# Six tiles of 344 tokens in two interleaved streams over one weight ring, for a hybrid decoder layer on eight cores

## The reference, cut to what matters

```python
D_MODEL = 1024; BATCH = 8; SEQ = 2048; DEC_BATCH = 128; PLE_DIM = 256
GLA_HEADS = 4; GLA_DV = 128; GLA_DK = 64; GLA_RANK = 16; CONV_WIDTH = 512; D_FF = 2816

def swiglu(x, w_gate, w_up, w_down):
    return (jax.nn.silu(x @ w_gate) * (x @ w_up)) @ w_down

def token_mixer(u, s0, conv0, w_in, w_gate_up, b_gate, gla_norm_g, conv_w, w_out):
    z = u @ w_in
    q, k, v, g, r, cb, cc, ch = jnp.split(z, points, axis=-1)
    gate_logit = (r @ w_gate_up + b_gate)
    log_a = jax.nn.log_sigmoid(gate_logit) / GLA_GATE_NORM
    o, s_new = gla_chunked(q, k, v, log_a, s0)   # S_t = diag(a_t) S_{t-1} + k_t^T v_t, o_t = q_t S_t
    o = rms_norm(o, gla_norm_g) * jax.nn.silu(g)
    full = jnp.concatenate([conv0, cc * ch], axis=1)
    y = sum(conv_w[j] * full[:, j:j + t_len] for j in range(CONV_K))
    out = jnp.concatenate([o, cb * y], axis=-1) @ w_out
    return out, s_new, full[:, -(CONV_K - 1):]

def decoder_layer(x, p, s0, conv0, ng, ...):
    h = x + 0.5 * rms_norm(swiglu(rms_norm(x, ng[0]), f1_gate, f1_up, f1_down), ng[1])
    mix, s_new, conv_new = token_mixer(rms_norm(h, ng[2]), s0, conv0, ...)
    h = h + rms_norm(mix, ng[3])
    h = h + 0.5 * rms_norm(swiglu(rms_norm(h, ng[4]), f2_gate, f2_up, f2_down), ng[5])
    gate = jax.nn.sigmoid(rms_norm(h, ng[6]) @ w_ple_gate)
    return h + rms_norm((p @ w_ple_proj) * gate, ng[7]), s_new, conv_new
```

## Time and profile before

| | |
|---|---|
| median of 3 runs | 2049.12 us (2028.93 to 2090.03) |
| span of the profiled execution, slowest core (core 5) | 2001.6 us |
| spans of the eight cores | 1986.7 to 2001.6 us |
| PE busy | 1718.5 us, 8,050 matmuls |
| DVE, ACT, POOL busy | 779.6, 657.8, 240.2 us |
| moved by DMA | 417.88 MB, mean 209 GB/s |

### The profile page before, as it was taken

How to read it: one execution, slowest core, us unless ns; L and a number is a source line. 1 busy time by engine, 2 the same in 40 slices (tenths; PEclk the granted TensorE clock), 3 DMA queues, 4 the chain that set the end, 5 groups by cost and what they waited for, 6 DMA issues and landing times.

```text
span 2001.6 us, 24196 instructions; the slowest of 8 cores (1986.7 to 2001.6 us)
## 1 busy us (share of the span) xinstructions
PE 1718.5 (86%) x8050; PEld 1375.0 (69%) x8050; DVE 779.6 (39%) x1338; ACT 657.8 (33%) x1274; POOL 240.2 (12%) x458
## 2 busy tenths in 40 slices
PE   5997879978988789979979789859997967799985
PEld 4885768856866668747858678647885757678865
DVE  2514526245513445045413355144513444234134
ACT  2124452253123441262233432352224341222243
POOL 1110101110110111101110111100110101001110
PEclk9997989989997899979988899979997985599986
DMA  9984759858893559849874558754663658346644
GB/s 257 312 254 122 201 155 297 253 173 253 285 279 106 168 185 296 256 162 289 261 222 158 189 203 255 225 179 169 219 195 114 206 198 273 138 148 224 189 140 143
DMA packets 77918, 417.88 MB, mean 209 GB/s; under 512 B 11203, under 2 KB 11860, under 8 KB 42726
## 3 DMA queue, kind: packets, MB, share of 16 engines
q0 software_dynamic: 65264, 396.88, 63.5%
q1 hardware_dynamic: 12534, 19.45, 3.5%
HBM read 405.55 MB, written 10.75 MB: 208 GB/s over the span
## 4 chain that ended last, share of the span: by engine, by line
PE 76%; ACT 8%; DVE 6%; issue 5%; DMA 3%; DVEq 0%; POOL 0%; ACTq 0%; POOLq 0%
PE ps_bank L287 66%; PE ps_bank L612 5%; PE ps_bank L300 3%; DMA sb_wslot<-f1a 3%; ACT sb_tmpa L318 2%; PE ps_bank L970 1%; ACT sb_sq L318 1%; DVE sb_big L321 1%; ACT sb_rs L318 1%; ACT sb_hgb L697 1%; DVE sb_xn L451 1%; ACT sb_xn L477 1%; DVE sb_Sst L326 1%; DVE sb_tmpb L326 1%; DVE sb_om L321 1%
## 5 line engine op out<-in xcount | busy, mean ns | idle before, releaser
L287 PE MATMUL ps_bank<-sb_xn,sb_wslot 128*128 128x512 f32 (+1 forms) x3456 | 829.1, 397 | 19.8 <-DVE sb_tmpa L321 10.4
L287 PEld LDWEIGHTS ps_bank<-sb_xn,sb_wslot 128*128 128x128 f32 x3456 | 653.2, 197 | 169.9 <-issue 27.0
L287 PE MATMUL ps_bank<-sb_big,sb_wslot 128*128 128x512 f32 x1408 | 336.4, 397 | 0.0
L287 PEld LDWEIGHTS ps_bank<-sb_big,sb_wslot 128*128 128x128 f32 x1408 | 262.0, 188 | 61.1
L318 ACT ACTIVATE sb_tmpa<-sb_tmpa 128x512 f32<-128x512 f32 (+1 forms) x216 | 133.4, 618 | 427.2 <-DVE sb_tmpa L321 427.0
L451 DVE TENSOR_TENSOR sb_xn<-sb_xn,sb_rs 128x512 fp32r<-128x512 f32 (+1 forms) x104 | 65.9, 644 | 489.4 <-ACT sb_rs L318 467.0
L321 DVE TENSOR_TENSOR sb_tmpa<-ps_bank,sb_rs 128x512 f32<-128x512 f32 (+1 forms) x216 | 144.6, 670 | 201.3 <-ACT sb_rs L318 126.2
L321 DVE TENSOR_TENSOR sb_tmpb<-ps_bank,sb_rs 128x512 f32<-128x512 f32 x176 | 121.2, 689 | 149.0 <-PE ps_bank L287 149.0
L612 PE MATMUL ps_bank<-sb_xn,sb_wslot 128*128 128x512 f32 x384 | 109.6, 453 | 45.1 <-DMA sb_wslot<-f1a 23.7
L321 DVE TENSOR_TENSOR sb_big<-sb_tmpb,sb_tmpa 128x512 fp32r<-128x512 f32 x176 | 121.9, 692 | 38.5 <-ACT sb_tmpa L318 24.4
L612 PEld LDWEIGHTS ps_bank<-sb_xn,sb_wslot 128*128 128x128 f32 x384 | 85.1, 224 | 69.0 <-issue 47.8
(11 more groups left out here) (130 smaller groups left out, 1483.6 us busy)
## 6 DMA issues: line engine op xcount, KB each, us to landing
sb_wslot<-f1a POOLq DMA_DIRECT2D x88, 1024.0 KB, 8.3
sb_wslot<-f2a POOLq DMA_DIRECT2D x88, 1024.0 KB, 6.9
sb_wslot<-f1b POOLq DMA_DIRECT2D x64, 704.0 KB, 5.6
sb_wslot<-f2b POOLq DMA_DIRECT2D x64, 704.0 KB, 5.5
sb_wslot<-wca POOLq DMA_DIRECT2D x20, 1024.0 KB, 6.5
sb_wslot<-wo POOLq DMA_DIRECT2D x20, 1024.0 KB, 6.8
sb_wslot<-wpg POOLq DMA_DIRECT2D x20, 1024.0 KB, 6.6
sb_wslot<-wv POOLq DMA_DIRECT2D x10, 1024.0 KB, 8.5
```

The source lines that it names most:

```text
L287: ins = e.matmul(out.ap, a.ap, b.ap, start=(first and i == 0), stop=(last and i == n_ - 1))
```

## The change

The 2,064 tokens of a core become six tiles of 344; the sample's 16 tokens are the last columns of the last tile, so they need no matmuls or weight fetches of their own in the projections. Tiles 0, 2, 4 are stream A, tiles 1, 3, 5 stream B, each with its own residual, normalised input and work buffer. Both run as Python generators, and a small scheduler with a made-up clock chooses whose next piece is recorded; B starts with a clock of `LAG` = 16. The weight sequence is gone through three times instead of four (and a part more). Each fetched tile is used by A and later by B, and its room is free when both have released it (`pump`, `get`, `release`). The ring takes what is left of the on-chip memory: 15,624 words per partition in the built program. Nothing is fetched over the end of the ring: what does not fit starts at 0.

Keys are projected once, and the token-major form comes from a transpose (`kz_build`). The normalised input is formed before the matmuls, so that the feed-forward needs one ACT and one DVE operation per weight tile and stream. Sums of squares go to a bank per stream (banks 0 and 1), all else rotates over six banks. The embedding gate uses Tanh in place of Sigmoid.

```diff
-TT = 512
 NTOK = SEQ + NS
-SLOT_W = 2048
-NSLOT = 5
+TILES = [344] * 6
+LAG = 16.0
 COMPUTE = ("pe", "act", "dve", "pool")
...
-    wk_d = din("wk", (128, 2048))
...
+        streams = []
+        for i, nm in enumerate("AB"):
+            streams.append(Stream(nm, P.sbuf("h" + nm, 128, 8 * NMAX), P.sbuf("xn" + nm, 128, 8 * NMAX),
+                                  P.sbuf("W" + nm, 128, WMAX), P.sbuf("rs" + nm, 128, NMAX),
+                                  [P.sbuf(f"sq{nm}{k}", 128, NMAX) for k in range(3)], banks[i]))
+        RW = nc.sbuf_bytes_remaining // 4 - 16
+        RW -= RW % 8
+        WR = P.sbuf("wring", 128, RW)
...
+            o = [(wg_d, 0, 2048), (wg_d, 1, 2048), (wca_d, 0, 2048), (wcb_d, 0, 1024), (wkq_d, 0, 2048), (wkq_d, 1, 2048),
+                 (wv_d, 0, 2048), (wv_d, 1, 2048)]
+            for c in range(1, 4):
+                o += [(wca_d, c, 2048), (wcb_d, c, 1024)]
+            return o + [(wo_d, m2, 2048) for m2 in range(4)]
...
+        order = (ffn_w(0) + mix_w() + ffn_w(1) + ple_w()) * (len(tiles) // 2)
+        place = []
+        wst = {"issued": 0, "pos": 0}
+        NWS = 16
+
+        def pump():
+            freed = min(s.rel for s in streams)
+            while wst["issued"] < len(order):
+                i = wst["issued"]
+                if i - freed >= NWS:
+                    return
+                d, blk, words = order[i]
+                lo = wst["pos"]
+                if lo + words > RW:
+                    lo = 0
+                if any(place[k][0] < lo + words and lo < place[k][1] for k in range(freed, i)):
+                    return
+                place.append((lo, lo + words))
+                wst["pos"] = lo + words
+                wst["issued"] += 1
+                dst = WR.v(lo, lo + words, r=True)
+                src = d[blk * 128:(blk + 1) * 128, :]
+                P.op("pool", (lambda o, s: lambda e: e.dma_start(out=o.ap, in_=s))(dst, src), writes=[dst], dma=f"ws{i % NWS}")
+
+        def get(S, d, blk):
+            i = S.wi
+            assert order[i][0] is d and order[i][1] == blk, (i, blk)
+            while True:
+                pump()
+                if i < wst["issued"]:
+                    break
+                yield None
+            S.wi += 1
+            base = place[i][0]
+            return lambda lo, hi: WR.v(base + lo, base + hi, r=True)
+
+        def release(S):
+            S.rel = S.wi
...
+        def cost(n, cnt):
+            return cnt * max(0.111, n * 0.4556e-3)
...
+        def ffn(S, T, f, gpost, gnext):
+            n = T.n
+            hid = lambda j: S.W.v(j * n, (j + 1) * n, r=True)
+            for j in range(NJ):
+                w = yield from get(S, fA_d[f], j)
+                bg_, bu_ = nb(), nb()
+                mm(bg_.v(0, n), [(w(k * 128, (k + 1) * 128), xv(S, k, n)) for k in range(8)])
+                mm(bu_.v(0, n), [(w(1024 + k * 128, 1024 + (k + 1) * 128), xv(S, k, n)) for k in range(8)])
+                release(S)
+                t = ta().v(0, n)
+                act(t, bg_.v(0, n), AF.Silu)
+                tt(hid(j), bu_.v(0, n), t, ALU.mult)
+                yield cost(n, 16)
+            pend = []
+            for m in range(8):
+                bk = nb(True)
+                for half in range(2):
+                    w = yield from get(S, fB_d[f], 2 * m + half)
+                    mm(bk.v(0, n), [(w(kk * 128, (kk + 1) * 128), hid(half * 11 + kk)) for kk in range(11)],
+                       first=(half == 0), last=(half == 1))
+                    release(S)
+                    if half == 0:
+                        flush(S, T, pend, 0)
+                    else:
+                        evac(S, T, m, bk, gpost, True, pend)
+                        drop(bk)
+                    yield cost(n, 11)
+            yield from boundary(S, T, pend, make_mul_fo(S, T), gnext)
...
-            slk = wget(wk_d, 0)
-            for s in range(nsub):
-                tok = lambda k: Ref("xn", k * TT, k * TT + n, xn.t[:, k * TT + s * rows: k * TT + (s + 1) * rows].bitcast(F32R))
-                bkk = nb()
-                mm(bkk.v(0, 256, 0, rows), [(tok(k), slk.v(k * 256, (k + 1) * 256, r=True)) for k in range(8)])
-                if is_sample:
...
+            def kz_build(lo, hi):
+                c = hi - lo
+                bt = nb()
+                transposes([(bt.v(pp * 128, (pp + 1) * 128, 0, c), wv_(S, T, "kt", pp * n + lo, pp * n + hi, r=False), ident()) for pp in range(2)],
...
+        progs = [stream_prog(streams[0], tiles[0::2]), stream_prog(streams[1], tiles[1::2])]
+        clock = [0.0, LAG]
+        alive = [True, True]
+        while any(alive):
+            first = 0 if (alive[0] and (not alive[1] or clock[0] <= clock[1])) else 1
+            ran = False
+            for k in (first, 1 - first):
+                if not alive[k]:
+                    continue
+                try:
+                    v = next(progs[k])
+                except StopIteration:
+                    alive[k] = False
+                    streams[k].rel = len(order)
+                    ran = True
+                    break
+                if v is not None:
+                    clock[k] += v
+                    ran = True
+                    break
```

More of the change, by code:

```diff
@@ L258, in build_program @@
[L258 to L265 removed]
+        tas = [P.sbuf(f"ta{i}", 128, 512) for i in range(3)]
+        tbs = [P.sbuf(f"tb{i}", 128, 512) for i in range(2)]
+        attms = [P.sbuf(f"attm{i}", 128, 512) for i in range(2)]
+        osqs = [P.sbuf(f"osq{i}", 128, 512) for i in range(2)]
+        ucxs = [P.sbuf(f"ucx{i}", 128, NMAX + 2) for i in range(2)]
@@ L1036, in build_program @@
+        assert all(s.wi == len(order) for s in streams)
         P.finish_waits("sp")
```

1238 lines of the change are left out of this document (540 added, 698 removed).

## The result

The changed kernel takes 3,291.8 us (median of 4 runs, 3,288.9 to 3,328.2) where the kernel before takes 2,055.4 (4 runs, 2,028.9 to 2,090.0). Over the even runs the changed kernel takes 1.62 times the time before, 95% interval 1.59 to 1.64 (the two medians alone give 1.60). Forecast were 2,935 us, 2,600 to 3,400: the measured time lies in that range, but above the 2,750 to 3,250 us that the prediction gave its own mechanism.

The account below looks back on a forecast made before the run. TensorE was taken as the bound, 86% busy. Work 1,441 + exposed fetch waits 1,022 + clock loss 315 + rest 110 = 2,888 us of span, plus 47 around it: 2,935 us, range 2,600 to 3,400.

Parts of the forecast that it names:

- The mechanism of the waits: Feed-forwards: A's seven-tile lead fills the seven-tile ring, so TensorE waits out whole fetches, 175 exposed; 2,750 to 3,250 us, chance 0.65.
- 47 us around the span: Added to the forecast span because the runs' median before lay 47 us above the profiled span.
- rival 1: The clock stays at 0.50 through every burst, costing 810 us instead of 315: 3,430 us; chance 0.13.
- TensorE's work, 1,441 us: All matmuls after the change at full clock: 8,592 of 344 columns at 157.1 ns, 1,350 us, and 766 others, 91 us.
- The passes of DVE and ACT: One pass each per weight tile and stream, 465 ns on DVE and 425 on ACT, hidden under TensorE's 2.51 us group.
- The waits, 1,022 us: Exposed weight fetches: 102 of 1 MB at 6.2 us, 73 of 704 KB at 5.2, 10 us for pairs; ends 950 and 1,285.
- rival 2: Waits shorter than every row, 1,8 us less each under the lighter load: 2,620 us; chance 0.15.
- The clock, 315 us: Each of 175 matmul bursts starts at half clock after its gap and loses 1.8 us; low end 263.
- The rest, 110 us (60 to 200): Start 24 us, A's first tiles 9, B's uncovered end 25, mixer chains mostly under the other stream's matmuls 50.
- Rival 3: Faster: fetches go out before the matmuls the rows name, so waits are hidden, 1,600 us; chance 0.04.
- the turning point at 2.6 us: The change gains if each of 175 waits, with its clock loss, costs less than 2.6 us.
- The sign of the forecast: The changed kernel is slower than before: chance 0.95 slower, 0.04 faster by over 2%, 0.01 within 2%.

Follow-up runs that it names:

- lag0: The changed kernel with LAG 0 in place of 16 and no cap on stream A's lead: 2,189.2 us.
- lead3: The changed kernel, LAG still 16, with stream A allowed a weight tile in a feed-forward only if fewer than three tiles ahead of B: 2,012.0 us.
- warm: The changed kernel with 32 or 26 matmuls on constants added where stream A's next weight tile has only just been asked for in a feed-forward: 3,066.6 us.
- ring5_lead3: lead3 with the ring cut from 15,624 to 10,240 words, five tiles: 2,244.2 us.
- LAG 0: The changed kernel with LAG 0 and A's lead capped at three tiles: 1,951.1 us; with a third residual buffer as well, 1,931.5 us.
- lead5: lead3 with stream A's lead capped at five tiles in place of three: 2,016.0 us.
- LAG 5: The changed kernel with LAG 5 and A's lead capped at three tiles: 1,975.9 us; with a third residual buffer as well, 1,896.1 us.

## Why the prediction came out as it did

**The mechanism of the waits was right, and what stood beside it was not.** The comb of 32 matmuls and a gap that ends with a landing in the ring, the clock (0.76 to 0.785 on the eight cores), DMA's share of the chain (29%, "about a third"), the rate (91 GB/s, "under 110") are all as described, and lag0 and lead3 show that the lead of seven tiles in a ring of seven makes it. That the time fell inside the range is in part luck. Its upper end of 3,400 was built from waits of 1,285 us, a rest of 200 and 47 us around the span; the waits were 994, the 47 were not there, and a rest of 479 us filled the room that they had left. By the time alone rival 1 with its 3,430 us was nearer than the forecast with 2,935; only the trace parts them.

**TensorE's work, 1,441 us: right as a price, by lead3,** where dense groups cost 157.8 ns per matmul. (The prediction counts 8,031 matmuls before where the page has 8,050; at its price the 19 are 2 us.) The passes of DVE and ACT measure 517 and 456 ns (465 and 425 in the prediction) and stay hidden.

**The waits, 1,022 us: right.** Of the prediction's 1,022 us, 175 x 0.16 = 28 are tails that the trace counts as busy; 994 remain, and the trace shows 1,003 of idle time behind all DMAs, 9 of them at the start. The fetch of 1 MB lands in 5.2 us (5.4 predicted), that of 704 KB in 4.6 (4.4), and 6.02 and 4.99 us of idle time stand against 6.04 and 5.04. Against the middle of the earlier trace rows, 5.8 us, that is 0.6 us less under the lighter load, and rival 2 with its 1.8 us falls. The Trainium skill (DMA: Bandwidth & Descriptors, Latency and other measured facts) has a smaller fixed cost at lighter load; the trace agrees with the direction. One caution on the earlier trace rows, which the prediction calls a fetch that TensorE waited out: TensorE did other matmuls beside more than half of it and was idle for 3.0 us before 1662.90. The 0.54 and 0.13 us between the matmul, the issue and the landing are not touched by that.

**The clock, 315 us: too small, but within its ends.** Groups by shape, busy us of the changed kernel and then of lead3, which has the same matmuls without the comb:

```profile
L335 PE MATMUL ps_bank<-sb_xnA,sb_wring 128*128 128x344 f32 x2784 | 727.7, 440 | 638.5 <-DMA sb_wring<-f2a 296.1
...
L335 PE MATMUL ps_bank<-sb_WA,sb_wring 128*128 128x344 f32 x1296 | 348.8, 440 | 379.9 <-DMA sb_wring<-f2b 189.1
...
L335 PE MATMUL ps_bank<-sb_xnB,sb_wring 128*128 128x344 f32 x2784 | 523.2, 344 | 38.1 <-DVE sb_xnB L371 30.4
...
L335 PE MATMUL ps_bank<-sb_WB,sb_wring 128*128 128x344 f32 x1296 | 250.4, 345 | 6.4 <-DVE sb_WB L793 3.4
```

```profile
L336 PE MATMUL ps_bank<-sb_xnB,sb_wring 128*128 128x344 f32 x2784 | 502.3, 335 | 70.0 <-DVE sb_xnB L372 57.1
L336 PE MATMUL ps_bank<-sb_xnA,sb_wring 128*128 128x344 f32 x2784 | 496.4, 333 | 50.9 <-DVE sb_xnA L372 38.6
...
L336 PE MATMUL ps_bank<-sb_WB,sb_wring 128*128 128x344 f32 x1296 | 242.1, 336 | 4.8 <-DVE sb_WB L800 3.5
L336 PE MATMUL ps_bank<-sb_WA,sb_wring 128*128 128x344 f32 x1296 | 230.5, 325 | 9.3 <-DMA sb_WA<-p 9.3
```

The sums are 1,850.1 and 1,471.3: 379 us, of which 28 are tails, so 351 us, 2.0 us a burst where I took 1.8 (ends 263 and 385). Nearly all of it, 350 of 379 us, is in A's groups: the comb's bursts lose 2.2 us there (4.72 us for 2.51), and B's group, a few microseconds later, runs at almost full rate (2.77 us). That is why rival 1 gave too much: cold is the half of each burst that follows the gap. The Trainium skill (TensorE: Matmul & The Clock Gate, Loop structure matters more than you think) draws a wait for DMA ahead of every matmul, which then runs cold; the trace agrees for the 16 matmuls behind the gap and not for the 16 after them. The warm experiment, in which 380 us of matmul time came back with the waits left in place, shows the loss to be real and apart from the wait.

**The rest, 110 us (60 to 200): this is the step that failed.** 3,293.0 - 1,441 - 994 - 379 = 479 us are left. 283 us of it are idle time, mostly behind squares, normalised input and attention rows (237.7 us in five rows), and some 196 us are busy time above the dense price, the part that lead3 has too (1,624 - 1,441 = 183): cold starts behind those gaps, sums with no neighbour. The step that failed is the sentence that a normalisation of one stream is mostly under the other's matmuls, put at 50 us: I had no row for it, and lead3 shows the gaps without the comb (302.7 us in five rows). The profile of before had the scale: its own span less its matmuls at dense price is at least 2,001.6 - 1,612 = 390 us. A normalisation now has 344 columns in place of 512, but there are six tiles in place of four. That 390 us would have been a better start than a sum from nothing; with it in place of 110 the forecast of the span comes to about 3,170 us. Some of the 479 us belongs to this one core and not to the kernel: core 1 was granted 0.81 in stretches, and core 6 of the same run, which never was, has a span of 3,237.2 us, the same 379 us of clock and tails (against lead3's core 5), about 955 us of waits for DMAs, and 462 us left.

**The 47 us around the span** were not there: this run took 3,294.6 us with a span of 3,293.0, and in every run whose cores are on record the time is within 3 us of the longest span. The median of before lay above its profiled span because other runs were slower, not because something of that size lies around a span. The two errors have opposite signs: the span was missed by 405 us (2,888 against 3,293), the time by 357.

**Rival 3's price was wrong in the same step.** Without the waits the kernel takes not 1,600 but 2,012 us. One exposed fetch costs (3,292 - 2,012)/185 = 6.9 us in all (7.7 by lag0, 8.5 by ring5_lead3), and at LAG 16 the change had next to nothing to give without them: lead3's 2,012.0 us against 2,018.6 of the kernel before beside it, 7 us or one exposed fetch. The prediction had put the turning point at 2.6 us for each of 175. The sign of the forecast was safe, its margin was not understood.

**What stays open:** how the offset of about one to two tiles gains its 25 to 40 us (fewer uncovered sums than at LAG 16, fewer table loads, and cover that LAG 0 has not); the runs show the gain and the gaps, and do not part the three. Nor was the rest of some 380 us that lead3 keeps idle taken apart further than by its rows of waits.

## What to carry to other kernels

Where two consumers share a ring, compare the lead of the first with the depth of the ring before anything else: at equality each fetch is issued only when its user is next in line, and the cost here was the whole landing plus a cold start, about 7 to 8.5 us. Here two tiles of slack removed it (lead5), and more brought nothing (lead3). And size the "rest" of a forecast by the kernel at hand, its span less its dense work, then ask what the change takes from that; here a second stream did not hide a normalisation by being there; that its matmuls must be recorded into that very gap is what I conclude, and LAG 5 is the only run that points to it.
